# Sums of squares in a two-stack transformer kernel: four tiles added on GpSimd, the last pair handed over tile by tile

## The reference, cut to what matters

```
def rms_norm(x, gain):
    xf = x.astype(jnp.float32)
    y = xf * lax.rsqrt(jnp.mean(xf * xf, axis=-1, keepdims=True) + NORM_EPS)
    return (y * gain.astype(jnp.float32)).astype(x.dtype)
```

## Time and profile before

| | |
|---|---|
| Time, 3 runs | 2577.83, 2578.78 (median), 2583.71 us |
| Span of the profiled execution | 2580.4 us (the page has no other time of this execution) |
| PE busy | 2369.4 us, 92% |
| DVE busy | 1498.5 us, 58% |
| ACT busy | 1021.1 us, 40% |
| POOL busy | 0.2 us, 4 instructions |
| Mean granted TensorE clock | 0.938 of full |
| DMA | 436.26 MB, mean 169 GB/s |

### The profile page before, as it was taken

How to read it: one execution, slowest core, us unless ns; L and a number is a source line. 1 busy time by engine, 2 the same in 40 slices (tenths; PEclk the granted TensorE clock), 3 DMA queues, 4 the chain that set the end, 5 groups by cost and what they waited for, 6 DMA issues and landing times.

```text
span 2580.4 us, 44727 instructions
## 1 busy us (share of the span) xinstructions
PE 2369.4 (92%) x17136; PEld 2203.8 (85%) x17136; DVE 1498.5 (58%) x2564; ACT 1021.1 (40%) x1670; POOL 0.2 (0%) x4
## 2 busy tenths in 40 slices
PE   5799899988798899989899999899978899998998
PEld 4687699987686799979899978799966799897998
DVE  4433177745441477836677776577766554666544
ACT  3312244414231344325544444444444544455443
POOL 0000000000000000000000000000000000000000
PEclk8898799998898899999899999899989899998999
DMA  4343179962433299844289854299842366442664
GB/s 127 91 112 102 33 251 289 290 192 83 123 83 99 77 291 292 271 127 129 85 273 291 289 165 127 86 292 286 276 114 82 115 181 185 127 132 85 194 186 131
DMA packets 553295, 436.26 MB, mean 169 GB/s; under 512 B 31824, under 2 KB 479352, under 8 KB 553080
## 3 DMA queue, kind: packets, MB, share of 16 engines
q1 hardware_dynamic: 549840, 431.35, 55.2%
q10 hardware_dynamic: 3368, 3.71, 0.5%
HBM read 433.96 MB, written 1.05 MB: 169 GB/s over the span
## 4 chain that ended last, share of the span: by engine, by line
PE 85%; DVE 7%; ACT 3%; issue 1%; DMA 1%; DVEq 1%; ACTq 1%; SPq 0%
PE bank L575 12%; PE bank L576 12%; PE bank L577 12%; PE acc L575 6%; PE acc L576 6%; PE acc L577 6%; PE bank L561 5%; PE bank L702 5%; PE acc L620 3%; PE bank L980 2%; PE bank L779 2%; PE bank L585 1%; PE bank L570 1%; PE bank L691 1%; PE bank L745 1%
## 5 line engine op out<-in xcount | busy, mean ns | idle before, releaser
L575 PE MATMUL bank<-h_hi,w_hi 128*128 128x256 f32 x2704 | 787.4, 291 | 28.1 <-DVE h_lo L1251 16.1
L576 PE MATMUL bank<-h_lo,w_hi 128*128 128x256 f32 x2704 | 774.6, 286 | 0.0
L577 PE MATMUL bank<-h_hi,w_lo 128*128 128x256 f32 x2704 | 774.1, 286 | 0.0
L1013 ACT ACTIVATE w_hi<-wslot 128x1024 fp32r<-128x1024 f32 x510 | 529.8, 1054 | 527.9 <-PE acc L577 312.6
L1429 DVE TENSOR_TENSOR w_lo<-wslot,w_hi 128x1024 fp32r<-128x1024 f32 x396 | 473.2, 1221 | 263.0 <-ACT w_hi L1013 262.8
L575 PEld LDWEIGHTS bank<-h_hi,w_hi 128*128 128x128 f32 x2704 | 527.9, 195 | 46.9 <-issue 31.9
L576 PEld LDWEIGHTS bank<-h_lo,w_hi 128*128 128x128 f32 x2704 | 529.9, 196 | 0.0
L577 PEld LDWEIGHTS bank<-h_hi,w_lo 128*128 128x128 f32 x2704 | 528.8, 196 | 0.0
L575 PE MATMUL acc<-mid_hi,w_hi 128*128 128x256 f32 x1056 | 302.2, 286 | 0.5 <-DVE mid_lo L1662 0.5
L577 PE MATMUL acc<-mid_hi,w_lo 128*128 128x256 f32 x1056 | 298.7, 283 | 0.0
L576 PE MATMUL acc<-mid_lo,w_hi 128*128 128x256 f32 x1056 | 298.7, 283 | 0.0
(11 more groups left out here) (255 smaller groups left out, 2742.9 us busy)
## 6 DMA issues: line engine op xcount, KB each, us to landing
wslot<-in_ada_w_dram SPq DMA_DIRECT2D x192, 512.0 KB, 5.8
wslot<-in_ffn_w_gate_dram SPq DMA_DIRECT2D x88, 512.0 KB, 4.7
wslot<-in_ffn_w_up_dram SPq DMA_DIRECT2D x88, 512.0 KB, 5.4
wslot<-in_ffn_w_down_dram SPq DMA_DIRECT2D x88, 512.0 KB, 3.4
wslot<-in_w_in_dram SPq DMA_DIRECT2D x72, 512.0 KB, 4.0
wslot<-in_sb_w_in_dram SPq DMA_DIRECT2D x48, 512.0 KB, 4.5
wslot<-in_w_ffn_gate_dram SPq DMA_DIRECT2D x44, 512.0 KB, 4.9
wslot<-in_w_ffn_up_dram SPq DMA_DIRECT2D x44, 512.0 KB, 5.6
```

The source lines that it names most:

```text
L575: pe.matmul(dst, w_hi[:, w, cols], hi, start=start, stop=False, skip_group_check=True)
L576: pe.matmul(dst, w_hi[:, w, cols], lo, start=False, stop=False, skip_group_check=True)
L577: return pe.matmul(dst, w_lo[:, w, cols], hi, start=False, stop=stop, skip_group_check=True)
L1013: return act.activation(dst, src, ACT.Copy)
```

## The change

Two things are done.

The first: DVE hands x over in five pieces (tiles 0-1, 2-3, 4-5, 6, 7) and ACT squares the same five. x_ready and squares count five in each phase in place of four. The fourth and fifth DVE piece wait for the same event, the end of the last product.

The second: GpSimd gets a block. In each norm it adds the squares of tile 1 to those of tile 0 as soon as the first square is counted, those of tile 3 to tile 2 behind the second, waits until both adds are counted (sq_pairs), and adds tile 2 to tile 0 (counted in sq_added). PE does five matmuls instead of eight: tiles 4 and 5, the sum in tile 0, tile 6, tile 7, in this order, so it waits for the third square first, then for sq_added, then for the fourth and fifth square.

```diff
--- before.py
+++ after.py
@@ -107,6 +107,7 @@
 N_SLOTS = 15
 PART_DOWN = 4
 PART_LAST = 2
+TILE_GROUPS = ((0, 2), (2, 4), (4, 6), (6, 7), (7, 8))
 
 
 def split_index(what, f):
@@ -146,7 +147,7 @@
         return {f"{k}{n}": u for n, u in enumerate(uses) for k in ("slot", "high", "unit_done")}
 
     def norm(split="", **more):
-        counts = dict(squares=4, sumsq=1, rstd=1)
+        counts = dict(squares=5, sq_pairs=2, sq_added=1, sumsq=1, rstd=1)
         if split != "ffn" or more["stack"] == 1:
             counts.update(h_ready=KT)
         if more["gain"][0] == "two":
@@ -166,7 +167,7 @@
         phase("att", counts, att=kind, n=n, **more)
 
     def add(**more):
-        phase("add", dict(x_ready=4, tiles_done=3), **more)
+        phase("add", dict(x_ready=5, tiles_done=3), **more)
 
     def ffn(ada=None, **more):
         counts = dict(silu_ready=NF, mid=NF, mid_high=NF, mid_ready=NF, up_done=NF, down_done=NF,
@@ -177,7 +178,7 @@
         phase("ffn", counts, ada=ada, **more)
         return start
 
-    phase("setup", dict(x_ready=4))
+    phase("setup", dict(x_ready=5))
     for l in range(DEPTH):
         norm(gain=("attn", l), split="att", att="da", layer=l)
         if l == 0:
@@ -192,7 +193,7 @@
         ada_at = ffn(ada=l, layer=l, stack=1)
         add(gate=None, last=("down_done", 0))
         phase("ada_units", {}, ada=l, start=ada_at)
-        phase("ple", dict(ple_t=1, ple_tc=1, ple_s=KT, ple_d=KT, x_ready=4,
+        phase("ple", dict(ple_t=1, ple_tc=1, ple_s=KT, ple_d=KT, x_ready=5,
                           **slots(SLOT_SMALL + 2, [4] * 2), **slots(SLOT_PLE, [4] * 2)), layer=l, start=ada_at)
         phase("ada_end", {}, ada=l, start=ada_at)
     ada_at = None
@@ -773,10 +774,12 @@
                 g = lambda k: at.get(k, 0)
                 full = lambda n: 16 * (g(f"slot{n}") + g(f"extra{n}") + 1)
                 if kind == "norm":
-                    for k in range(KT):
-                        if k % 2 == 0:
-                            pe.wait_ge(sem["squares"], g("squares") + k // 2 + 1)
-                        mm = pe.matmul(B(0, 0, 256), C("ones"), sqT[:, k, :], start=(k == 0), stop=(k == KT - 1))
+                    for k in (4, 5, 0, 6, 7):
+                        if k == 0:
+                            pe.wait_ge(sem["sq_added"], g("sq_added") + 1)
+                        elif k != 5:
+                            pe.wait_ge(sem["squares"], g("squares") + {4: 3, 6: 4, 7: 5}[k])
+                        mm = pe.matmul(B(0, 0, 256), C("ones"), sqT[:, k, :], start=(k == 4), stop=(k == KT - 1))
                     mm.then_inc(sem["sumsq"], 1)
                     clear_acc()
                 elif kind == "att":
@@ -1135,10 +1138,9 @@
                     if ph["split"] == "ffn":
                         for n in range(2):
                             high(SLOT_FF + n, n, 16 * (g(f"slot{SLOT_FF + n}") + 1))
-                    for q in range(4):
-                        act.wait_ge(sem["x_ready"], g("x_ready") - 3 + q)
-                        act.activation(sqT[:, 2 * q:2 * q + 2, :], xT[:, 2 * q:2 * q + 2, :], ACT.Square)\
-                           .then_inc(sem["squares"], 1)
+                    for q, (lo, hi) in enumerate(TILE_GROUPS):
+                        act.wait_ge(sem["x_ready"], g("x_ready") - 4 + q)
+                        act.activation(sqT[:, lo:hi, :], xT[:, lo:hi, :], ACT.Square).then_inc(sem["squares"], 1)
                     act.wait_ge(sem["sumsq"], g("sumsq") + 1)
                     inverse_root(rs[:, :], B(0, 0, 256), D).then_inc(sem["rstd"], 1)
                     if ph["split"]:
@@ -1245,6 +1247,19 @@
                                .then_inc(sem["ple_s"], 1)
 
 
+        @block.gpsimd
+        def _(pool):
+            for kind, at, _ in phases:
+                if kind == "norm":
+                    squares, added = at.get("squares", 0), at.get("sq_pairs", 0)
+                    for q in range(2):
+                        pool.wait_ge(sem["squares"], squares + q + 1)
+                        pool.tensor_tensor(sqT[:, 2 * q, :], sqT[:, 2 * q, :], sqT[:, 2 * q + 1, :], ALU.add)\
+                            .then_inc(sem["sq_pairs"], 1)
+                    pool.wait_ge(sem["sq_pairs"], added + 2)
+                    pool.tensor_tensor(sqT[:, 0, :], sqT[:, 0, :], sqT[:, 2, :], ALU.add).then_inc(sem["sq_added"], 1)
+
+
         @block.vector
         def _(dve):
             def stt(out, x, scalar, y, op0=ALU.mult, op1=ALU.mult):
@@ -1255,8 +1270,8 @@
             dve.memset(epst[:, :], EPS)
             dve.memset(attm[:, :, :], 0.0).then_inc(consts_ready, 1)
             dve.wait_ge(x_turned, 1)
-            for q in range(4):
-                dve.tensor_copy(xT[:, 2 * q:2 * q + 2, :], acc[:, 2 * q:2 * q + 2, :]).then_inc(sem["x_ready"], 1)
+            for lo, hi in TILE_GROUPS:
+                dve.tensor_copy(xT[:, lo:hi, :], acc[:, lo:hi, :]).then_inc(sem["x_ready"], 1)
             dve.wait_ge(params_turned, 1)
             for n, r in enumerate((P, N_B, 96, 96)):
                 last = dve.tensor_copy(pcol[:, n, 0:r], B(2, P * n, P * n + r))
@@ -1633,17 +1648,16 @@
                     name, freed = ph["last"]
                     done = slot_used[int(name[4:])] if name[:4] == "slot" else \
                         unit_done[int(name[9:])] if name[:4] == "unit" else sem[name]
-                    for q in range(4):
+                    for q, (lo, hi) in enumerate(TILE_GROUPS):
                         if q < 3:
                             dve.wait_ge(sem["tiles_done"], g("tiles_done") + q + 1)
                         else:
                             dve.wait_ge(done, g(name) + freed)
                         if ph["gate"] is None:
-                            last = dve.tensor_tensor(xT[:, 2 * q:2 * q + 2, :], xT[:, 2 * q:2 * q + 2, :],
-                                                     acc[:, 2 * q:2 * q + 2, :], ALU.add)
+                            last = dve.tensor_tensor(xT[:, lo:hi, :], xT[:, lo:hi, :], acc[:, lo:hi, :], ALU.add)
                         else:
                             l, part = ph["gate"]
-                            for m in (2 * q, 2 * q + 1):
+                            for m in range(lo, hi):
                                 last = stt(xT[:, m, :], acc[:, m, :], mod[:, l, 8 * part + m:8 * part + m + 1], xT[:, m, :],
                                            ALU.mult, ALU.add)
                         last.then_inc(sem["x_ready"], 1)
@@ -1692,8 +1706,8 @@
                             dve.tensor_tensor(sqT[:, bass.ds(2 * i + b, 1), :], silu_g[:, b:b + 1, :], bank[:, 2 * b + 1:2 * b + 2, 0:256],
                                               ALU.mult).then_inc(sem["ple_d"], 1)
                     dve.drain()
-                    for q in range(4):
-                        dve.tensor_tensor(xT[:, 2 * q:2 * q + 2, :], xT[:, 2 * q:2 * q + 2, :], sqT[:, 2 * q:2 * q + 2, :],
+                    for lo, hi in TILE_GROUPS:
+                        dve.tensor_tensor(xT[:, lo:hi, :], xT[:, lo:hi, :], sqT[:, lo:hi, :],
                                           ALU.add).then_inc(sem["x_ready"], 1)
                 elif kind == "store":
                     dve.wait_ge(x_turned, 2)
```

## The result

The ratio of the changed kernel to the one before is 1.0024, 95% interval 1.0014 to 1.0034; medians of 19 runs each, 2585.78 and 2580.57 us. The profiled execution took 2585.37 us, its span is 2583.6.

The account below looks back on a forecast made before the run. PE was taken to bound the kernel (85% of the chain of waits), each norm by the end of its ones matmuls. -6.5 (matmuls) + 2.7 (GpSimd beside DVE) + 1.0 (clock) = -2.8 gave 2576.0 us, range 2572.0 to 2583.0.

Parts of the forecast that it names:

- matmuls: Five instead of eight ones matmuls per norm, started at the third square, save 6.5 us over the 12 norms.
- GpSimd beside DVE: GpSimd's adds and DVE's w_lo may be unable to read SBUF together; cost 0 to 5.5 us, taken as 2.7.
- clock: PE's longer idle time ahead of norms may lower its clock; cost 0 to 4 us, taken as 1, one norm.
- rival B: Every meeting of an add with w_lo costs a wait: 2578.8 us, or 2577.8 with the clock kept; chance 0.25.
- the turns I worked out: Adds and w_lo halves alternating on SBUF in six norms, costing 0.2 to 2.3 us each, 5.5 us in all.
- 1136, +2.3 in these turns: At the norm of 1136, alternating adds and w_lo halves make PE's last three matmuls end at 1142.5, +2.3 us.
- What a GpSimd add costs: One GpSimd add of squares was bounded by 0.42 and 1.2 us and taken as 0.69.
- rival C: Three adds in a row outlast PE's work on tiles 4 and 5; 2584.8 us with 0.95 us adds; chance 0.15.
- a mean under 0.8: Sign in the profile after: if the 36 GpSimd adds average under 0.8 us, adds too long are ruled out.
- My own sign of a wrong mechanism: PE waiting on GpSimd over 0.5 us in most norms, or L779 ends moving as written without the total.
- The split: Splitting the last pair of tiles for DVE and ACT brings the last square 0.1 us forward; taken as 0.
- Rival D: Norm gains are lost again at DMA waits in the PLE stages: +1.3, 2580.1 us; chance 0.05.

Follow-up runs that it names:

- e2: The changed kernel without GpSimd's adds and PE's wait for them, tiles 1 to 3 left out of the sum; 0.9997 of before, 2577.12 us.
- e1: The changed kernel with one wait more: DVE's w_lo starts only after GpSimd's third add; 0.9992 of before, 2576.68 us.
- e9: The changed kernel with seven unread matmuls ahead of six norms, w_lo free to start; 1.0014 of before, 2583.08 us.
- e6: e1 with seven matmuls that nobody reads ahead of six norms; 0.9976 of before, 2572.79 us.
- e7: The changed kernel with one GpSimd add (tile 3 onto 2), seven matmuls from the first square, w_lo waiting for the add; 0.9991 of before, 2575.25 us.
- e8: The kernel before with five matmuls that nobody reads ahead of six norms; 0.9982 of before, 2575.18 us.
- e3: The kernel before with only the split into five pieces and squares, eight matmuls in tile order, GpSimd unused; 1.0000 of before, 2578.39 us.
- e5: The changed kernel with PE taking the GpSimd sum last, after tiles 4 to 7; 0.9995 of before, 2577.87 us.
- e4: The changed kernel with two GpSimd adds (pairs only) and six matmuls; 1.0013 of before, 2581.23 us.

## Why the prediction was wrong

The sum was -6.5 (matmuls) + 2.7 (GpSimd beside DVE) + 1.0 (clock) = -2.8. Measured is +5.2 us by the medians, +6.2 by the ratio, outside the range on the slow side. Two steps failed. The first is "GpSimd beside DVE ... I take 2.7, half": the runs show some 8 us. The second is the base under it, the matmuls with the clock, -6.5 + 1.0 = -5.5: e2, which has these two and nothing else, shows -0.8.

- **GpSimd beside DVE, taken as 2.7, bounds 0 and 5.5.** Shown to be 8.3 us (e1 against the changed kernel, interval 5 to 12) and 9.8 (e9 against e6, 6 to 14), at or above my upper bound. That a held add costs PE was in the text, as rival B; its size was not. Three things were wrong in the turns I worked out.
  - I let add and w_lo go in turn, so that an add would wait for one half of w_lo. In the norms of 1660, 2019 and 2220 the third add waits for both (2.86 or 2.87 us, w_lo undisturbed at 2.35), at 1498 the first add does; in those of 582, 1136 and 1874 a third add waits for one (1.58 or 1.59).
  - I took the starts of w_lo from before and let the third add at 1660 and 2019 go through at a cost of 0.2. By my own terms it is ready at 1662.12 (the second square ends at 1661.29, then 0.07, 0.69 and 0.07) and w_lo starts at 1662.11. A margin of that size is a coin toss; the bound had to hold both sides of it. The norms of 1660, 2019 and 2220 became 2.1, 2.1 and 3.5 us longer, and in this term I had put no number on 2220 at all. The start of w_lo moves, too: at 1498 it was 1.28 us behind the start of the first square, and is 0.37 in the changed kernel.
  - I let PE's last matmuls run at the full level behind the wait. At 2220 they take 2.93 us for six records, where 582 has 1.56 in e9: 1.4 of the 3.5 us lost there is clock, which the wait brought about. The two terms of the sum aren't independent, and 8.3 holds both.
- **1136, +2.3 in these turns, was luck.** It was measured at +2.5. But the add waited for one half only and ended 3.9 us after the first square's start, for 5.1 in the turns; the rest is matmuls at the low clock.
- **What the rule on sharing said.** The Trainium skill (SBUF — State Buffer, "Who interferes with whom") says that the two hold a shared interface for whole instructions and that the order of issue decides who is blocked. The trace agrees where an add waits for one instruction: 1.58 us beside w_lo, 0.73 alone. It agrees for the other direction: where an add stands inside w_lo's time, at 582, 1136 and 1874, w_lo takes 3.26, 3.27 and 3.31 for two where it takes 2.35. It doesn't tell of the 2.87: at 1660 the second half of w_lo began 1.06 us after the add was ready, and still went first. I had this rule and gave it half its price.
- **What a GpSimd add costs, taken as 0.69.** Measured 0.726 to 0.730 alone (e1, e6, e7). Right, so rival C's cause, an add that is too long by itself, falls. Its sign didn't tell this: I had said that a mean under 0.8 rules C out, and the mean in the changed kernel is 1.06, because held adds count in it; it took e1. The Trainium skill's figure (GPSIMD Engine Reference, "Performance versus the Vector engine"), scaled to an estimate of 0.56 us plus a fixed part, agrees if that part is 0.17.
- **My own sign of a wrong mechanism came.** It was a wait of PE on GpSimd of over 0.5 us in most norms; it is 0.8 to 2.4 us in 7 of 12.
- **The matmuls, -6.5.** At 325 and 878 -0.45 each (-0.5 foreseen), 1289 and 2371 -0.2 and -0.3 (-0.3), the first norm -1.45 (-2.0), 582 -1.3 (-1.1): right. But the -0.6 at 1660 and 2019 supposed that the clock rises when it rose before, and e2 has +0.8 there, and +1.95 at 1136, all at the low level; 1498, at the full one by chance of the moment, has -1.9. In all, e2 is at 0.9997: about -0.8 us (interval -3.4 to +1.8) where -5.5 was foreseen. With the clock held up, e6 is at 61.4 for e8's 62.6 in the sums and 0.9976 for 0.9982, a difference of 1.5 us that the intervals don't bear out. So even there the -6.5 isn't seen.
- **The clock, taken as +1.0, bounds 0 and +4.** I only asked what would get worse, and the earlier trace rows showed that the kernel before already paid. Holding the level up gives back 4.1 us behind the adds (e6 against e1) and 4.6 in the kernel before (e8). That is what the low level costs in either; how much of it the change added can't be told from these two, nor be parted from the matmuls in e2.
- **The split, taken as 0.** Right (e3: 1.0000).
- **Rival D** (gain given back at a PLE transfer) is out: that wait was 12.2 and is 11.9.

Added up again with what was measured: -0.8 (e2) and 8.3 (adds held) give +7.5; measured were +5.2 and +6.2, with intervals of 2.6 us on the first term and 3.6 on the second.

That w_lo and the adds hold each other up, and that this is on PE's chain, is shown by kernels that change one thing (e1, e5, e9 against e6). That filling PE's idle time ahead of a norm brings its clock back is shown too (e6 against e1, e8 against before). That the idle time alone decides is not: at 1498 PE stood idle 2.40 us in e2 and stayed at the full level, and 1.33 in before and fell in the midst of the matmuls. Why a waiting add gets in between the two halves of w_lo in some norms and not in others is not settled. The time since w_lo's start is not it: the add came 0.07 us behind it at 1660 and 0.76 in e4 at 2220 and waited for both, 0.60 at 1136 and waited for one. Where it got in, w_lo had begun while an earlier add was still running and had been held itself (3.26 at 582, 3.27 at 1136, 3.31 at 1874); that is a pattern of one profile, and no run tried it by itself.

## What to carry to other kernels

A helper operation on GpSimd is priced by what DVE does at that time, not by its own 0.73 us: one wait that keeps it apart from w_lo was worth 8 us here, more than the whole change was to bring. Order PE's work so that what depends on the helper comes last; this alone took back the loss (e5), without touching the conflict. And work taken away from PE ahead of a wait can come back as a lower clock: before removing matmuls from such a place, read its granted clock, since here filling the idle time (e8, -0.18%) was worth at least as much as removing three of eight matmuls (e2, -0.03%).

## What the runs showed of the hardware that was not expected

- Matmuls that nobody reads, 1.36 us of them ahead of six norms, made the kernel before 4.6 us faster (e8). At 2019 the ones matmuls behind such filling ran at 1.00 of the clock in e6, at 0.50 in e1 without it: 2.42 us for 4.63.
- A GpSimd add that came 0.07 us behind two back-to-back DVE operations waited for both of them (2.86 us for 0.73), though it was ready 1.06 us before the second began.
- The time of one and the same kernel spreads by 0.7% (before: 2569.75 to 2586.98 in 35 runs) on one core, and it goes with the mean granted clock: over these 35 runs the clock lies between 0.933 and 0.943, the correlation is -0.91, and a clock lower by 0.001 comes with 1.7 us more. That is an order found among runs, not an experiment.
